# One of six conditioning groups computed in the expert stage and not in the mixer's levels

## The reference

```python
def reference(x, ..., c_2, ctx_2, c_ctx_2, ada_w_2, ada_b_2, norm_w_2, ...):
    x = first_block(x, norm1_g, w_in, ..., peer_wq, peer_keys, peer_u, peer_v, normf_g)
    return second_block(x, c_2, ctx_2, c_ctx_2, ada_w_2, ada_b_2, norm_w_2, ...)

# first_block: h = rmsnorm(x); p = h @ w_in; gated delta rule and mLSTM (the mixer);
#              x = x + y @ w_out; h2 = rmsnorm(x); x = x + _peer(h2, ...); rmsnorm(x)
def _peer(h, w_q, sub_keys, u_tab, v_tab):       # the experts, per token and head
    qry = (t @ w_q)...                            # 8 heads, 2 x 128
    scores = einsum(qry, sub_keys)                # 2 x 128 keys; top 16 of each, top 16 of 256 sums
    act = gelu(einsum(tb, u_tab[idx]))            # 128 rows of u for each token
    out = einsum(gate * act, v_tab[idx])          # 128 rows of v for each token

# second_block, two layers i = 0, 1 (pooling mixer, then attention mixer), each with
    sh1, sc1, g1, sh2, sc2, g2 = split(silu(c) @ ada_w[i] + ada_b[i], 6)
    csh1, ..., cg2 = split(silu(c_ctx) @ ada_w[i] + ada_b[i], 6)
    # they scale, shift and gate the layer's tokens (x) and the context's tokens (ctx)
```

## Time and profile before

| | |
|---|---|
| median of 3 runs | 1699.68 us (1692.08 to 1699.78) |
| the profiled execution | 1682.63 us, its span 1680.8 us |
| PE, DVE, POOL, ACT busy in the span | 89%, 66%, 49%, 35% |
| mean granted clock of PE | 0.945 of full speed |
| read from HBM | 474.65 MB |

### The profile page before, as it was taken

One profiled execution on the slowest core, in us unless ns is written; L12 is line 12 of the kernel. 1 busy time (PEld: TensorE's weight loads), 2 busy tenths in 40 slices (PEclk: granted clock), 3 DMA queues, 4 the chain that ended last, 5 costly groups with the idle time before them and its releaser, 6 DMA issues.

```text
span 1680.8 us, 22334 instructions
## 1 busy us (share of the span) xinstructions
PE 1492.1 (89%) x8384; PEld 1067.5 (64%) x8384; DVE 1104.9 (66%) x2162; ACT 583.3 (35%) x846; POOL 828.5 (49%) x746
## 2 busy tenths in 40 slices
PE   8999999756566699999887976989999999999999
PEld 7997675644212266665343432438998886699987
DVE  4865533798498867876756765327886536568865
ACT  6653331211121221232000011227664434466652
POOL 0025220476767765655777777633764101227650
PEclk9999999987677799999999997999999999999999
DMA  7447860698999999999999999985555525735551
GB/s 279 151 151 305 312 248 25 232 387 303 398 407 364 406 389 402 403 403 403 407 402 398 409 392 409 401 334 173 178 201 176 199 92 211 265 136 188 171 198 47
DMA packets 154251, 477.15 MB, mean 284 GB/s; under 512 B 10016, under 2 KB 12320, under 8 KB 150944
## 3 DMA queue, kind: packets, MB, share of 16 engines
q0 software_dynamic: 73728, 268.47, 40.9%
q1 hardware_dynamic: 80416, 207.27, 33.7%
HBM read 474.65 MB, written 1.05 MB: 283 GB/s over the span
## 4 chain that ended last, share of the span: by engine, by line
PE 55%; DMA 13%; DVE 11%; POOL 9%; issue 4%; ACT 2%; DVEq 0%; ACTq 0%; POOLq 0%
PE ps L673 54%; DMA arena<-in_peer_v,cl 10%; POOL arena L2795 7%; DVE arena L1855 2%; DMA wring<-in_peer_v,cl 2%; POOL wring L2795 2%; PE ps L677 1%; DVE arena L1470 1%; DVE arena L1476 1%; DVE wring L1855 1%; DMA wring<-in_peer_u,arena 1%; DMA wring<-in_ada 0%; DVE cvb L1476 0%; DVE arena L1473 0%; DVE arena L1785 0%
## 5 line engine op out<-in xcount | busy, mean ns | idle before, releaser
L673 PE MATMUL ps<-arena,wring 128*128 128x256 f32 (+2 forms) x2360 | 599.7, 493 | 103.4 <-DMA arena<-in_peer_v,cl 99.8
L673 PEld LDWEIGHTS ps<-arena,wring 128*128 128x128 f32 (+1 forms) x2360 | 330.2, 166 | 353.5 <-DMA arena<-in_peer_v,cl 180.4
L1855 DVE CUSTOM_DVE_ANT_0 arena<-arena 128x1024 f32<-128x1024 f32 x214 | 257.2, 1225 | 134.4 <-DMA arena<-in_peer_u,arena 131.3
L2795 POOL DMA_INDIRECT arena<-in_peer_u,arena x214 | 245.1, 1145 | 190.3 <-DVE arena L1813 78.0
L2795 POOL DMA_INDIRECT arena<-in_peer_v,cl x214 | 227.6, 1063 | 78.2 <-issue 58.5
L673 PE MATMUL ps<-hhl,wh 128*128 128x256 f32 (+1 forms) x1056 | 252.4, 322 | 1.2 <-POOL hhl L2805 0.7
L2190 ACT ACT_TABLE_LOAD x64 | 82.1, 1283 | 397.2 <-DVE arena L1855 269.7
L1470 DVE TENSOR_TENSOR wl<-wring,wh 128x2048 fp32r<-128x2048 f32 (+1 forms) x76 | 168.1, 2211 | 57.3 <-ACT wh L2193 55.5
L673 PE MATMUL ps<-hhl,wl 128*128 128x256 f32 x704 | 198.4, 282 | 0.0
L673 PEld LDWEIGHTS ps<-hhl,wh 128*128 128x128 f32 x1056 | 175.6, 190 | 19.6 <-POOL hhl L2805 2.5
L2193 ACT ACTIVATE wh<-wring 128x2048 fp32r<-128x2048 f32 (+1 forms) x78 | 146.1, 1873 | 70.9 <-PE ps L673 69.0
(11 more groups left out here) (261 smaller groups left out, 2049.1 us busy)
## 6 DMA issues: line engine op xcount, KB each, us to landing
wring<-in_ups SPq DMA_DIRECT2D x33, 2048.0 KB, 9.8
wring<-in_ada SPq DMA_DIRECT2D x24, 2048.0 KB, 9.8
wring<-in_ffn_w_down SPq DMA_DIRECT2D x12, 2048.0 KB, 7.9
wring<-in_w_in SPq DMA_DIRECT2D x8, 2048.0 KB, 8.3
wring<-in_ffn_w_down SPq DMA_DIRECT2D x6, 1536.0 KB, 7.4
wring<-in_peer_wq SPq DMA_DIRECT2D x4, 2048.0 KB, 15.0
wring<-in_attn_w_qkv SPq DMA_DIRECT2D x4, 2048.0 KB, 8.3
wring<-in_w_out SPq DMA_DIRECT2D x2, 2048.0 KB, 9.5
```

The costliest lines, as they stand in the source:

```text
L673: return pe.matmul(o, l, r, start=start, stop=stop)
L1855: ve.tensor_tensor_reduce(out=o, in0=o, in1=h2[:, t, :], scale=1.0, scalar=0.0, op0=MUL, op1=ADD, accum_out=dots[j % 2][:, k:k + 1]).then_ ...
L2795: po.indirect_dma_start(out=ring[n % NR], out_offset=None, in_=table, in_offset=bass.IndirectOffsetOnAxis(ap=which, axis=0)).then_inc(S[f" ...
```

## The change

Group 3 is taken out of the mixer (`GROUPS_MIXER` 3, `LOADS_MIXER` 12) and done in the expert stage, between the last scores and the transposes of the context's tokens. Its four loads stand in SP's queue behind the queries' weights, and use the three slots in turn. PE does its eight units in two steps, leaves one step free, and does the small matmuls in a fourth. ACT and VectorE have their parts at the same place. PSUM bank 7 stays out of the ring of banks until the group is done. A third name, `p_adc`, counts these units on the same semaphore.

```diff
--- before.py
+++ after.py
@@ -104,7 +104,7 @@
     GOES_ON = {
         "p_gp": ("p_hT", 4), "p_h2T": ("p_gp", 1), "p_xc": ("p_h2T", 4), "p_zb": ("p_xc", 4), "p_xT": ("p_zb", 1), "p_cum": ("p_g", 1), "p_crow": ("p_cum", 1),
         "p_em": ("p_crow", 1), "p_ym": ("p_mo", 8), "p_s0": ("p_ym", 2), "p_s1": ("p_s0", 2), "p_s2": ("p_s1", 2), "p_qs": ("p_s2", 2),
-        "p_go": ("p_s3", 2), "p_hy": ("p_go", 2), "p_wo": ("p_hy", 2), "p_wom": ("p_ada", 16), "p_adb": ("p_wom", 4), "p_kq": ("p_kk", 4), "p_dd": ("p_kq", 4),
+        "p_go": ("p_s3", 2), "p_hy": ("p_go", 2), "p_wo": ("p_hy", 2), "p_wom": ("p_ada", 12), "p_adc": ("p_wom", 4), "p_adb": ("p_adc", 4), "p_kq": ("p_kk", 4), "p_dd": ("p_kq", 4),
         "p_la": ("p_dd", 4), "p_q": ("p_pj", 16), "p_sc": ("p_tok", 4), "p_cpl": ("p_l2", 2), "p_pl": ("p_cpl", 4),
         "p_cu": ("p_mb", 8), "p_cd": ("p_dec", 8), "p_dn": ("p_cd", 24), "p_ckv": ("p_ms", 4), "p_hs": ("p_ckv", 3),
         "p_lb": ("p_lt", 20), "p_vt": ("p_lb", 4), "p_s": ("p_cu", 22), "p_pt": ("p_q", 10), "p_o": ("p_sc", 10), "p_y": ("p_o", 8),
@@ -180,7 +180,7 @@
     rows_ada = cvb[0].rearrange("p i n -> p (i n)")
     still = cvb[1].rearrange("p i n -> p (i n)")[:, 0:256]
     sc32_late = gt[:, 0:256].rearrange("p (k n) -> p k n", k=8)
-    LOADS_EARLY, GROUPS_EARLY = 16, 4
+    LOADS_MIXER, LOADS_EARLY, GROUPS_MIXER, GROUPS_EARLY = 12, 16, 3, 4
 
     def area(at, n):
         return arena[:, at:at + n]
@@ -591,7 +591,7 @@
             if n == 2:
                 sp.dma_start(cl[:, :], a["c_levels"]).then_inc(S["d_l"], 16)
         free[3] = [("p_pj", 16)]
-        for i in range(LOADS_EARLY):
+        for i in range(LOADS_MIXER):
             load(("ada", i), ("p_ada", i + 1), (lambda ap: ap, a["ada"][i]), slot=(2, 0, 1, 3)[i % 4])
         for half in range(2):
             load(("wo", half), ("p_wo", OUT_LAST.index((half, 1)) + 1), kcols(a["w_out"][0], 512 * half, 512), slot=2 - 2 * half)
@@ -603,6 +603,8 @@
         sp.dma_start(flat(keyT), a["keys"]).then_inc(S["d_k"], 16)
         for q in range(1, 4):
             load(("wq", q), ("p_q", 2 * q + 4), kcols(a["peer_wq"][0], 512 * q, 512), n=3)
+        for i in range(LOADS_MIXER, LOADS_EARLY):
+            load(("ada", i), ("p_adc", i - LOADS_MIXER + 1), (lambda ap: ap, a["ada"][i]), n=3)
         sp.wait_ge(*at("a_sc", 10))
         sp.dma_start(xin, a["ctx_2"][0].rearrange("(t p) d -> p t d", p=128)).then_inc(S["d_xc"], 16)
         sp.wait_ge(*at("v_h2", 2))
@@ -852,7 +854,7 @@
         proj(5)
         l2(0, 1)
         pe.wait_ge(*at("a_c16", 1))
-        cond = conditioning(range(GROUPS_EARLY), sc32, "p_ada", 1)
+        cond = conditioning(range(GROUPS_MIXER), sc32, "p_ada", 1)
         proj(6)
         l2_rows(0, 1)
         pe.wait_ge(*at("a_conv", 2))
@@ -1107,6 +1109,16 @@
                 yield from first_queries(h, 1)
             for h in range(2, 8):
                 yield from queries(h)
+            cond = conditioning(range(GROUPS_MIXER, GROUPS_EARLY), sc32, "p_adc", 0)
+            for _ in range(2):
+                for _ in range(4):
+                    next(cond)
+                yield
+            yield
+            next(cond)
+            held[7] = "a_ad", GROUPS_EARLY
+            ring8[0] = [0, 1, 2, 3, 4, 7]
+            yield
             pe.wait_ge(*at("d_xc", 16))
             for t in range(2):
                 for q in range(2):
@@ -1219,7 +1231,7 @@
                     k.then_inc(S["p_zb"], 1)
                 yield what[0]
 
-        ring8[0] = [0, 1, 2, 3, 4, 7]
+        ring8[0] = list(range(5))
         woven(peer(), context())
 
         def r(ap):
@@ -1631,7 +1643,7 @@
                         seq(tt(PB[:, s, :], PG[:, s, :], vcols("pb", 8), MUL))
                 yield
 
-        cond = conditioning(range(GROUPS_EARLY), 9)
+        cond = conditioning(range(GROUPS_MIXER), 9)
         for _ in range(2):
             next(cond)
 
@@ -1907,8 +1919,11 @@
             return k
 
         def context():
-            for _ in range(18):
+            for _ in range(21):
                 yield
+            for _ in conditioning(range(GROUPS_MIXER, GROUPS_EARLY), 0):
+                pass
+            yield
             ve.wait_ge(*at("a_xc", 4))
             seq(ve.memset(hpc_c[:, :, 0:8], 0.0))
             seq(ve.memset(hpc_c[:, :, 264:272], 0.0))
@@ -2317,14 +2332,15 @@
             for g in groups:
                 for _ in range(wait):
                     yield
-                ac.wait_ge(*at("p_ada" if g < GROUPS_EARLY else "p_adb", 4 * (g % GROUPS_EARLY) + 4))
+                ac.wait_ge(*(at("p_ada", 4 * g + 4) if g < GROUPS_MIXER else at("p_adc", 4) if g < GROUPS_EARLY
+                             else at("p_adb", 4 * (g - GROUPS_EARLY) + 4)))
                 if g > 0:
                     ac.wait_ge(*at("p_ads", g))
                 told(copy(rows_ada, bank_ada), "a_ad", g + 1)
                 yield
                 yield
 
-        cond = conditioning(range(GROUPS_EARLY), 8)
+        cond = conditioning(range(GROUPS_MIXER), 8)
         for _ in range(2):
             next(cond)
 
@@ -2774,7 +2796,7 @@
             told(k, "g_bv", h + 1)
 
 
-        po.wait_ge(*at("p_ada", LOADS_EARLY))
+        po.wait_ge(*at("p_ada", LOADS_MIXER))
         told(po.memset(slots[3][:, 0:2048], 0.0), "g_zero", 1)
         for n, (kind, t, m) in enumerate(ROWS):
             if kind == "u":
```

## The result

| | before | after |
|---|---|---|
| median of 20 runs each | 1695.07 us (1689.65 to 1700.63) | 1703.53 us (1700.56 to 1708.84) |
| ratio, 95% interval | | 1.0044 (1.0033 to 1.0055) |
| the same in a later set: 22 and 5 runs | 1681.87 us | 1692.53 us, 1.0070 (1.0056 to 1.0083) |

By the ratios the kernel is 7.5 us slower in the first set of runs and 11.8 in the second; 3.0 was forecast, in a range from -10 to +13. The intervals of the two sets do not touch, so there is no one number for the change. (A 23rd run of before in the later set took 2386.96 us at a mean granted clock of 0.553 and is left out.) The forecast of 1702.7 us lies within 1 us of the measured 1703.5 by luck: it stood on a median of three runs, 1699.68, and that of 20 runs is 4.6 us lower, about as much as the change was forecast too small.

The account below looks back on a forecast made before the run. PE's work was taken to bound the mixer's levels, and nearly full DMA engines (403 GB/s) most of the expert stage. -8.5 + 9.0 + 0 + 2.5 = +3.0 on 1699.7 gave 1702.7 us, range 1690 to 1713.

Parts of the forecast that it names:

- Term 1: Mixer levels: without group 3's eight units and four `pick` matmuls, all up to the first gather comes earlier; -8.5 us.
- Term 2: Expert stage: four loads take 20.8 us of DMA time, holes cover 10.4 and 1.4; +9.0 us.
- meet much the same parts: Hole at 480 to 520 us: the context's pooling still meets much the same parts of `topk`; 4.0 us hole left unchanged.
- Term 3: PE among the gathers: 8.8 us of matmuls and about 5 us waiting for the fourth load are hidden; 0.
- Term 4: End of the expert stage: the context's last steps come four steps later, delaying ACT and VectorE; +2.5 us.
- A: Expert stage: the loads are hidden, bytes do not set the stage's end; 1691 to 1694 us, chance 0.14.
- B: 340 to 400 us: first two loads delay u rows, VectorE and its indices, so PE's queries; +13.4, 1713 us, chance 0.15.
- C: Last five pairs: last gathers are issued late and the backlog stays; +7 in place of +2.5, 1707 us, chance 0.10.
- D: Mixer's shorter levels: ACT's copies take PE's place, so nothing is gained; +11.5, 1711 us, chance 0.06.

Follow-up runs that it names:

- e1: Before with the fourth group left out of the whole kernel, four tiny matmuls carrying its semaphores, context's old step numbers; -9.5 us against before (0.9944).
- e2: After without the group's four weight loads in the expert stage, its units still run; -3.2 us against before (0.9981).
- e10: e2 with e7's turn of the PSUM banks: units without loads, no wait for VectorE's addition; -4.0 us against before (0.9976).
- e7: After with the PSUM bank turn moved on, so the context's fourth group of transposes need not wait for VectorE's addition; +5.7 us against before (1.0034).
- e5: Before with four empty steps ahead of the context's tokens on PE, VectorE and ACT; +2.0 us against before (1.0012).
- e9: After, unchanged, run and profiled again in a later set; +11.8 us against before (1.0070).
- e12: Before, unchanged, run and profiled again in the same set as e9; +0.5 us against before (1.0003).
- e3: After with its four loads, but each of the group's units one tiny matmul in place of four full ones; +7.5 us against before (1.0044).
- e4: After's group done earlier, inside the queries' steps, loads in slots that come free earlier, context's old step numbers; -3.0 us against before (0.9982).
- e6: As e4, but three of the four loads land before the first gathers, two of them in ring rows still empty; -6.9 us against before (0.9959).
- e8: After with the context's steps from the eleventh on 5.4 turns apart in place of 5.6; +21.7 us against before (1.0129).
- e11: e8 with e7's turn of the PSUM banks; +16.3 us against before (1.0097).

## Why the prediction held, and why its size was low

**Term 1, the mixer (-8.5): right.** -9.9 in the pair of profiles, -9.5 at the end (e1). The 0.3 us taken off for VectorE at the start of level five were not needed. A unit was also priced too low: the row of a level behind it took 1.09 us to the next start (217.38 to the unit at 218.47), where such rows without units take 0.9 (4.63 us for 40 records).

**Term 2, the bytes (+9.0): the size near, its reasons partly wrong.** Measured by taking the loads away: +10.7 (e2 against after) and +9.8 (e10 against e7). But the mark that I set for it, first to last gather longer by 5 to 12 us, is missed: the pair shows 22.4. That stretch also holds the four steps (+6.0 in e5, of which half comes back when the last rows land) and the wait for the bank. One profile of each kernel parts the 22.4 so: 10.3 with the loads (e7 over e10), which is inside the mark, 9.4 with the wait for the bank (e9 over e7), 2.7 for the rest (e10 over e12). Wrong was "I take none" for the delay by the first two loads: VectorE waited 3.8 us for u rows, over the 2 that the prediction gave as the sign, and 2.5 us of the lead were gone at turn 1. From the first gather to turn 1 it is 76.7 to 77.0 us in e12 and in the kernels without the loads there (e1, e2, e10), 79.0 to 79.9 with them (both profiles of after, e3, e7), and 84.3 in e4. And wrong was that the pooling, moved by four steps, would "meet much the same parts": in e5 the holes from 480 to 640 sum to 10.5 us in place of 5.2, in after (e9) to 13.1.

**Term 3, PE among the gathers (0): this is the step that failed.** What I counted was right: PE waits 6.4 us for the fourth load, no more for the tokens, and the matmuls cost nothing beside the loads (e3). What I did not count is the bank. `take` gave the fourth group of the context's transposes the PSUM bank that held the conditioning's columns, and VectorE, which has to read them first, comes to that only behind four u rows (the last begins at 471.12 in e9, the addition at 472.38). PE waits 8.9 to 9.3 us, and behind it stand the uses for which POOL's ring waits. That the wait makes POOL's pause and the holes behind it is shown by e7, where both are gone. Its price in time is less sure: 1.7 or 6.0 us by the after that e7 is compared with, 5.8 by the four kernels with either spacing and either bank, and 0.8, not clear of zero, where there are no loads (e10 against e2).

In the 1681 sets this explains most of what the forecast lacked. With term 1, the bytes and the steps put together, 9.5 us are left there (11.8 + 9.5 - 9.8 - 2.0), of which e7's line gives 6.0 back. In the 1694 sets it does not: there 4.3 us are left (7.5 + 9.5 - 10.7 - 2.0), and they are just what e2, without loads, has over e1 and the steps, where by e10 the wait costs next to nothing. e10 too, which has neither loads nor that wait, is 5.5 over e1, of which the steps are 2.0. These 3.5 to 4.3 us are near the intervals of the kernels compared (some 4 us), and stay open.

**Term 4, the end (+2.5): right.** +2.0 by the times of e5, which hold all that the four steps do and not the end alone. From the last use to the next block it is +2.5 to +3.3 in five profiles, and 4.7 and 5.0 in those of e2 and of after in the first set. The mark was that ACT's squares start 2.5 us later behind the last use; it was 1.8 in e9 and 3.1 in the first profile.

**Rivals.** A (1691 to 1694: the loads are hidden) is out by e2 against after. B (the first loads delay the indices) takes 2.5 us of the lead in after, and decides e4. C (a worse tail) had the place right, but only part of its price came. D (nothing gained in the mixer) is out by e1.

## What to carry to other kernels

A hole in the DMA engines is worth its bytes only if the engine that paces the stretch does not wait for what lands beside the new transfer: e4 filled the hole from 360 to 400 and lost 7 us at turn 1 by VectorE's waits for rows, while three of the four loads ahead of the first gather left all but 2.6 us of the mixer's gain standing (e6 against e1, some 4 us either way). When work is moved into a stream that takes its PSUM banks in turn, list which later `take` falls on the new bank and where its reader stands in the other engine's stream; the kernel's text has this wait in it before anything is timed. And spacing steps by a formula is not a free knob: 5.4 turns in place of 5.6 cost about 10 us (e8 over e9 9.9, e11 over e7 10.6, each pair with the banks alike but across two sets).

## What was not expected of the hardware

The same program differed by some 14 us between sets of runs (before: 1693.7 and 1695.1 in two sets, 1680.4 and 1681.9 in two). The profiles of after from a 1694 set and a 1681 set have spans of 1704.8 and 1690.7 us. Of the 14.1 us between them, 2.4 lie ahead of the first gather (303.7 and 301.3), 7.8 from there to the last use (833.2 and 825.4), 2.3 in the end of the stage and 1.5 in the rest (539.1 and 537.6). The cause stays open. A difference of chips is not shown: the record gives the chip of a set by a number, and 9 stands for the set of e1 to e4 (1693.7) as well as for that of e5 to e8 (1680.4), 12 for that of e9 to e12 (1681.9). The change itself cost 0.44% in one set and 0.70% in another, so a difference of half a per cent in this stage should be measured in more than one set, and kernels compared within one.
